# The differential stage as one stream over four heads, with a later tile's projection in pieces between the parts of each attention unit

## What is computed

```python
h = rms_norm(x, norm_g)
z = h @ w_in                        # 1024 -> 4096: ret_q,k,v,gate, diff_q,k,v,gate
# retention group: 4 heads of 128, in chunks of 128 rows with a recurrent state
# differential group: 4 heads; q and k are normed and rotated, in two maps of 64
s = einsum('bqhcd,bkhcd->bhcqk', q, k) * 64 ** -0.5      # c: the two maps, causal
p = softmax(s)
a = p[:, :, 0] - lam * p[:, :, 1]
o_diff = einsum('bhqk,bkhe->bqhe', a, v)
u = concat([rms_norm(o_ret) * silu(rg), rms_norm(o_diff) * (1 - lam_init) * silu(dg)])
y = x + u @ w_out
# sample rows: the same with 4096 cached keys and values each, in pages of 128 found by a table
```

## Time and profile before

| what | us |
| --- | --- |
| median of 3 runs | 2093.59 (2093.02 to 2105.36) |
| the profiled run, device time | 2095.8 |
| its span | 2094.1 |
| TensorE busy | 1702.9 (81%) |
| VectorE busy | 1124.7 (54%) |
| GpSimd busy | 702.4 (34%) |
| ScalarE busy | 675.1 (32%) |

### The profile page before, as it was taken

One profiled execution on the slowest core, in us unless ns is written; L12 is line 12 of the kernel. 1 busy time (PEld: TensorE's weight loads), 2 busy tenths in 40 slices (PEclk: granted clock), 3 DMA queues, 4 the chain that ended last, 5 costly groups with the idle time before them and its releaser, 6 DMA issues. The chain is left out here.

```text
span 2094.1 us, 31531 instructions
## 1 busy us (share of the span) xinstructions
PE 1702.9 (81%) x8316; PEld 1252.9 (60%) x8316; DVE 1124.7 (54%) x2194; ACT 675.1 (32%) x1964; POOL 702.4 (34%) x666
## 2 busy tenths in 40 slices
PE   5859779789799669578895888967889679549998
PEld 1238558568568458356683566845668456418887
DVE  2444533534524528678386783866838768472211
ACT  2321311311311312367233562235632357311100
POOL 1326436446356237211372113730127301140000
PEclk9879999999899889699996999968999789859999
DMA  8866575566566546330464313643136431343432
GB/s 304 302 218 188 165 224 182 178 208 194 168 215 196 181 143 201 120 109 29 133 202 121 106 31 119 201 126 106 42 104 196 131 111 51 84 147 130 136 134 72
DMA packets 185467, 314.54 MB, mean 150 GB/s; under 512 B 17331, under 2 KB 79548, under 8 KB 185156
## 3 DMA queue, kind: packets, MB, share of 16 engines
q1 hardware_dynamic: 176948, 287.22, 44.4%
q0 software_dynamic: 8352, 25.50, 3.2%
HBM read 275.99 MB, written 36.67 MB: 149 GB/s over the span
## 5 line engine op out<-in xcount | busy, mean ns | idle before, releaser
L540 PE MATMUL s_z<-g_w_hi,g_hT 128*128 128x512 f32 x1024 | 406.7, 397 | 43.6 <-DMA s_h_lo<-h_low_scratch 32.3
L542 PE MATMUL s_z<-g_w_hi,s_h_lo 128*128 128x512 f32 x1024 | 410.3, 401 | 0.0
L597 POOL TENSOR_TENSOR s_ring<-s_ring,s_q_row 128x1024 f32<-128x1024 f32 x128 | 321.1, 2510 | 257.3 <-DMA s_ring<-in_cache_k 245.0
L541 PE MATMUL s_z<-g_w_lo,g_hT 128*128 128x512 f32 x1024 | 406.1, 397 | 0.0
L603 DVE TENSOR_REDUCE s_scores<-s_ring 128x16 f32<-128x1024 f32 x128 | 156.2, 1220 | 332.1 <-POOL s_ring L597 320.1
L558 ACT COPY s_zqk<-s_z 128x256 f32<-128x256 f32 x128 | 47.7, 373 | 633.4 <-PE s_z L542 633.4
L540 PEld LDWEIGHTS s_z<-g_w_hi,g_hT 128*128 128x128 f32 x1024 | 195.4, 191 | 91.7 <-DMA s_h_lo<-h_low_scratch 35.5
L1262 ACT ACTIVATE s_weights<-s_sc,s_neg_max 128x512 f32<-128x512 f32 (+3 forms) x320 | 196.5, 624 | 91.4 <-DVE s_neg_max L1401 68.0
L541 PEld LDWEIGHTS s_z<-g_w_lo,g_hT 128*128 128x128 f32 x1024 | 195.4, 191 | 47.9
L542 PEld LDWEIGHTS s_z<-g_w_hi,s_h_lo 128*128 128x128 f32 x1024 | 195.1, 191 | 43.0
L1518 PE MATMUL s_o<-s_vg,s_aT 128*128 128x128 f32 x1088 | 159.8, 296 | 52.7 <-ACT s_aT L1244 48.3
(11 more groups left out here) (205 smaller groups left out, 2744.7 us busy)
## 6 DMA issues: line engine op xcount, KB each, us to landing
s_h_lo<-h_low_scratch SPq DMA_DIRECT2D x131, 512.0 KB, 3.5
s_ring<-in_cache_k SPq DMA_DIRECT2D x256, 256.0 KB, 3.3
s_ring<-in_cache_v SPq DMA_DIRECT2D x256, 256.0 KB, 2.9
w_raw<-in_w_in SPq DMA_DIRECT2D x8, 2048.0 KB, 11.4
s_w_raw<-in_w_in SPq DMA_DIRECT2D x64, 256.0 KB, 3.5
s_u_in<-u_scratch SPq DMA_DIRECT2D x17, 512.0 KB, 3.9
x_in<-in_x_prompt SPq DMA_DIRECT2D x16, 512.0 KB, 6.1
h_low_scratch<-lo_out POOLq DMA_DIRECT2D x16, 512.0 KB, 5.6
```

Of the source, the lines that this page charges most:

```text
L540: pe.matmul(s.z_bank[t % 2][:], hi, g.w_hi[:, c, :], start=(c == 0), stop=False)
L541: pe.matmul(s.z_bank[t % 2][:], hi, g.w_lo[:, c, :], start=False, stop=False)
L542: last = pe.matmul(s.z_bank[t % 2][:], lo, g.w_hi[:, c, :], start=False, stop=(c == DC - 1))
L597: pool.tensor_tensor(slot[:], slot[:], bc(s.q_row[:].unsqueeze(1), [P, 2, 512]), ALU.mult).then_inc(s.keys_times_q, 1)
```

## The change

The loop over heads in the differential stage becomes straight code: 64 tiles (`NTILE`) pass as one stream of steps from -5 to 65. In step n the engines work on the unit T = n and on the projection of tile X = n + 5 (`LEAD`), which may belong to the next head. TensorE does the projection in three pieces, of 3, 3 and 2 chunks, between the parts of the unit.

- One z bank and one turn bank take the place of two that served both.
- Keys' and values' slots become rings of 24 tiles (`VSLOTS`), as two heads overlap.
- Upper h no longer stays in SBUF after retention. Retention writes it to HBM (`h_high`) before its loop, and the differential stage loads both halves, 1 MB a tile, into three slots each. `g.hT` is laid out by tiles.
- The product of cached keys with q moves from GpSimd to VectorE (`use_keys`). Keys stand in steps 0 to 9 of each head (two pairs in the first six, then one), the row's softmax in 9 to 12, the values' eight quads in 12 to 15.
- The next head's weights are loaded whole in advance (`w_raw` holds 8 chunks) and split in steps 10 and 11, as each chunk of the old ones is used for the last time.
- In retention the loads of the next head's first three h tiles move from the loop's start to its end.

The diff, cut: declarations, the unchanged bodies that only lose their loop offset, and the removed code are left out.

```diff
-    rows = slice(t * P, (t + 1) * P)
     for c in range(DC):
-        hi, lo = g.hT[:, c, rows], s.h_lo[t % LSLOTS][:, c, :]
+        hi, lo = g.hT[:, t, c, :], s.h_lo[t % LSLOTS][:, c, :]
...
+            for t in range(LSLOTS):
+                load_low(sp, io, s, g, 0, t)
+            for t in range(NT):
+                sp.dma_start(io["h_high"][t], g.hT[:, t].rearrange("p c x -> p (c x)").bitcast(F32)).then_inc(high_stored, 16)
...
-                for t in range(LSLOTS):
-                    load_low(sp, io, s, g, it, t)
...
+                for t in range(LSLOTS):
+                    load_low(sp, io, s, g, it + 1, t)
+            sp.wait_ge(high_stored, 16 * NT)
+            for t in range(LSLOTS):
+                sp.wait_ge(g.low_loaded[t], low_at(s, NH, t))
...
+LEAD = 5
+NTILE = NH * NT
+UNIT_STEPS = range(-LEAD, NTILE + 2)
+VSLOTS = 24
+KEYS_AT = [2, 2, 2, 2, 2, 2, 1, 1, 1, 1] + [0] * 6
+QUADS_AT = [0] * 12 + [2, 2, 2, 2]
+FIRST_KEY = [sum(KEYS_AT[:i]) for i in range(NT)]
+FIRST_QUAD = [sum(QUADS_AT[:i]) for i in range(NT)]
...
+            def load_h(X):
+                if X >= NTILE:
+                    return
+                if X >= LSLOTS:
+                    sp.wait_ge(tile_used, X - LSLOTS + 1)
+                for dst, src in ((h_hi, "h_high"), (h_lo, "h_low")):
+                    sp.dma_start(dst[X % LSLOTS][:].rearrange("p c x -> p (c x)").bitcast(F32), io[src][X % NT]
+                                 ).then_inc(h_loaded[X % LSLOTS], 16)
+
...
+            for X in range(2):
+                load_h(X)
+            load_q(0)
+            for n in UNIT_STEPS:
+                load_h(n + LEAD + 2)
+                if n % 2 == 0 and 0 <= (n + 2) // 2 < NPAIRS:
+                    store_kv((n + 2) // 2)
+                h, i = row_step(n + 1)
+                if 0 <= h < NH:
+                    for j in range(FIRST_KEY[i], FIRST_KEY[i] + KEYS_AT[i]):
+                        load_pages(h, j)
+                    for j in range(2 * FIRST_QUAD[i], 2 * (FIRST_QUAD[i] + QUADS_AT[i])):
+                        load_pages(h, NPAIR + j)
+                    if h + 1 < NH and 1 <= i < 1 + DC:
+                        load_weights(h + 1, i - 1)
+                    if h + 1 < NH and i == 14:
+                        load_q(h + 1)
...
+            def keep_z(X):
...
+                act.wait_ge(tile_used, X + 1)
+                act.copy(zqk[b % 3][:, X % 2, :], z_bank[:, 0:2 * P])
+                act.copy(vg[:, X % VSLOTS, :], z_bank[:, 2 * P:4 * P])
+                act.activation(th[b % 2][:, X % 2, :], z_bank[:, 3 * P:4 * P], ACT.Tanh, scale=0.5).then_inc(z_kept, 1)
...
+            for n in UNIT_STEPS:
+                X, T, b = n + LEAD, n, (n + 2) // 2
+                new_head = (X + 1) // NT if (X + 1) % NT == 0 and X + 1 < NTILE else 0
+                for k in unit_groups(T - 2)[1]:
+                    keep_turned(("a", k))
+                if n % 2 == 0 and 0 <= b < NPAIRS:
+                    key_high(b)
+                h, i = row_step(n)
+                if i == 12 and 0 <= h < NH:
+                    act.wait_ge(row_dve, h * ROW_DVE + 4)
+                    act.activation(scores, scores, ACT.Exp, scale=QSCALE).then_inc(row_exp, 1)
+                if 0 <= T < NTILE:
+                    exps(T, 0)
+                if new_head:
+                    for c in range(0, 3):
+                        weights_high(new_head, c)
+                if 0 <= T - 2:
+                    square_output(T - 2)
+                if n % 2 == 1 and 0 <= n + 1 < NTILE:
+                    keep_turned(("k", (n + 1) // 2))
+                if 0 <= T + 1 < NTILE:
+                    keep_turned(("q", T + 1))
+                if new_head:
+                    for c in range(3, 6):
+                        weights_high(new_head, c)
+                if X < NTILE:
+                    keep_z(X)
+                    if X % 2 == 1:
+                        square(X // 2)
+                if new_head:
+                    for c in range(6, DC):
+                        weights_high(new_head, c)
+                for k in unit_groups(T - 1)[0]:
+                    keep_turned(("a", k))
+                if 0 <= T < NTILE:
+                    exps(T, 1)
...
+            def use_keys(h, j):
+                dve.wait_ge(q_loaded, 16 * (h + 1))
+                dve.wait_ge(ring_loaded[j % RING], ring_at(h, j))
+                slot = ring[j % RING]
+                chain.link(dve.tensor_tensor(slot[:], slot[:], bc(q_row[:].unsqueeze(1), [P, 2, 512]), ALU.mult))
+                dve.tensor_reduce(scores[:, 2 * j:2 * j + 2, :], slot[:].rearrange("p i (s f) -> p i s f", f=DH),
+                                  AX, ALU.add).then_inc(keys_used, 1)
...
+            for n in UNIT_STEPS:
+                X, T = n + LEAD, n
+                h, i = row_step(n)
+                new_head = (X + 1) // NT if (X + 1) % NT == 0 and X + 1 < NTILE else 0
+                now_head = X // NT if X % NT == 0 and 0 < X < NTILE else 0
+                keys = list(range(FIRST_KEY[i], FIRST_KEY[i] + KEYS_AT[i])) if 0 <= h < NH else []
+                if n % 2 == 1 and 0 <= (n + 3) // 2 < NPAIRS:
+                    square_sums((n + 3) // 2)
+                if 0 <= T < NTILE:
+                    find_bias(T, 0)
+                if 0 <= T + 1 < NTILE:
+                    split_q(T + 1)
+                if 0 <= T - 1 < NTILE:
+                    find_coef(T - 1)
+                    combine(T - 1)
+                if 0 <= T - 2:
+                    gate_output(T - 2)
+                if new_head:
+                    for c in range(0, 3):
+                        weights_low(new_head, c)
+                if now_head:
+                    for c in range(6, DC):
+                        weights_low(now_head, c)
+                if n % 2 == 0 and 0 <= (n + 2) // 2 < NPAIRS:
+                    key_low((n + 2) // 2)
+                if i == 0 and h >= 1:
+                    row_heads(h - 1)
+                if i == 12 and 0 <= h < NH:
+                    row_sums(h)
+                for j in keys[:1]:
+                    use_keys(h, j)
+                if 0 <= T < NTILE:
+                    find_bias(T, 1)
+                if n % 2 == 1 and 0 <= (n + 3) // 2 < NPAIRS:
+                    norm_and_rope((n + 3) // 2)
+                    halve_gate((n + 3) // 2)
+                if new_head:
+                    for c in range(3, 6):
+                        weights_low(new_head, c)
+                for j in keys[1:]:
+                    use_keys(h, j)
+                if 0 <= h < NH:
+                    if i == 9:
+                        row_largest(h)
+                    if i == 10:
+                        row_bias(h)
+                    if i == 11:
+                        row_shift(h)
+                if h >= 1:
+                    if i == 0:
+                        row_total(h - 1)
                     if i == 1:
+                        row_result(h - 1)
...
+            def project(X, chunks):
+                if X >= NTILE:
+                    return
+                h = X // NT
+                if chunks[0] == 0:
+                    if X >= 1:
+                        pe.wait_ge(z_kept, X)
+                    pe.wait_ge(h_loaded[X % LSLOTS], 32 * (X // LSLOTS + 1))
+                hi, lo = h_hi[X % LSLOTS], h_lo[X % LSLOTS]
+                for c in chunks:
+                    if X % NT == 0 and h >= 1:
+                        pe.wait_ge(w_low, (h - 1) * DC + c + 1)
+                    pe.matmul(z_bank[:], hi[:, c, :], g.w_hi[:, c, :], start=(c == 0), stop=False)
+                    pe.matmul(z_bank[:], hi[:, c, :], g.w_lo[:, c, :], start=False, stop=False)
+                    last = pe.matmul(z_bank[:], lo[:, c, :], g.w_hi[:, c, :], start=False, stop=(c == DC - 1))
+                    if c == DC - 1:
+                        last.then_inc(tile_used, 1)
+                    elif X % NT == NT - 1:
+                        last.then_inc(w_free, 1)
+
...
+            def turn(job):
+                kind, k = job
+                n = JOB[job]
+                if n >= 1:
+                    pe.wait_ge(turn_kept, n)
...
+            for n in UNIT_STEPS:
+                X, T = n + LEAD, n
+                h, i = row_step(n)
+                if 0 <= T < NTILE:
+                    score(T, 0)
+                project(X, range(0, 3))
+                turn_and_weigh(T - 2, unit_groups(T - 2)[1])
+                if 0 <= T < NTILE:
+                    score(T, 1)
+                if n % 2 == 1 and 0 <= n + 1 < NTILE:
+                    turn(("k", (n + 1) // 2))
+                project(X, range(3, 6))
+                if 0 <= h < NH:
+                    if i == 10:
+                        pe.wait_ge(row_dve, h * ROW_DVE + 1)
+                        pe.transpose(row_bank[0:HC, 0:P], row_max[:], g.ident[:]).then_inc(row_pe, 1)
+                    if i == 11:
+                        pe.wait_ge(row_dve, h * ROW_DVE + 3)
```

(13 more changed lines are left out.)

819 lines of the change are left out of this document (422 added, 397 removed).

## The result

The changed kernel takes 2024 us (median) against 2098 us for the kernel before on the same chip. The ratio is 0.9637, with a 95% interval of 0.9589 to 0.9686: faster by 3.6%. One of the changed kernel's four runs took 2116 us at a granted clock of 0.806, where the other three have 0.931 to 0.936, and the ratio leaves it out. The prediction was 2046 us, range 1992 to 2112, faster with a chance of 0.62.

The account below looks back on a forecast made before the run. TensorE's projection, waits in the attention units' ring over three engines, and 32 us of fill and drain per head were taken to bound the differential stage. Span 2094.1 - 62 (stage) + 15 (retention) = 2047, median 2046 us, range 1992 to 2112.

Parts of the forecast that it names:

- the prologue: Start of the differential stage: five steps with projection alone, 33 us, plus 2 for the first tile's two halves of h.
- the last head with the closing steps: End of the differential stage: 210 us for a head partly without projection, plus 13 for two closing steps.
- Steps 0 to 7: Narrow steps of each head: VectorE taken as the bound, 101 us together against 106 before.
- Sum 11.0, with waits 11.6 to 12: VectorE's time in us per narrow step: key pairs 5.1, unit work 3.8, norm, rope and the rest 2.1.
- the bound of 2.51 us: Narrow steps: upper price of one key product on VectorE, its time on GpSimd; 1.22 us was taken.
- Steps 8 to 15: Wider steps of each head: 63 us for 8 to 11 and 80 for 12 to 15, against 61 and 64.
- the walk: Differential stage: a step's time added up link by link through TensorE's in-order queue and ScalarE's copies, 20.9 us for unit 14.
- The rival that it would fall: Narrow steps: clock drops to 0.75, adding 67 us over 24 steps, 2113 us in all; chance 0.13.
- Longer hops: Differential stage: three more hand-overs, 0.75 us in each of 64 steps, add 48 us, giving 2094; chance 0.20.
- The product at GpSimd's price: Narrow steps: VectorE's key product costs 1.3 us more, 62 us in all, giving 2108; chance 0.05.
- the stream overlaps better than walked: Retention loads pass the stores, saving 15 us, and each stage step sheds 0.65, saving 42, giving 1990; chance 0.20.
- The stall: Retention's first head: 16 stores of h's upper half delay the fourth tile's load; 15 us, between bounds 0 and 27.

Follow-up runs that it names:

- e10: Changed kernel with VectorE's product of cached keys with q left out and put nowhere else; one run, differential stage 944 us against 952.
- e4: Changed kernel with a tile's eight chunks projected as one block instead of three pieces; ratio 1.0013 to the kernel before, stage 1038 us.
- e1: Changed kernel with the 16 stores of h's upper half issued on ScalarE's DMA queue instead of SP's; ratio 0.9568 to the kernel before.
- e6: e1 with the next head's first three loads moved back to the start of the retention loop; ratio 0.9566 to the kernel before.
- e5: Changed kernel loading only an eighth of h's lower half per tile after the first three in the differential stage; ratio 0.9615 to before.

## Why the prediction was right, and where its steps failed

**The direction and the bound.** That the change takes the gaps of the units and the 32 us of fill and drain, and that its pieces stand in TensorE's queue, was right; so were the prologue (35.6 us against 35) and the last head with the closing steps (221 against 223). Of the 38 us by which the stage came out shorter, all lie in the first three heads: 223.6 + 236.1 + 235.5 = 695 against 732.

**The first head.** Its steps 0 and 1 took 7.4 and 9.4 us, against 14.6 and 13.2 in the second, as no wide units lie before them: 11 us that the sum charged by taking three equal heads. Both facts stood in the prediction; the sum forgot one.

**Steps 0 to 7: right in size, wrong in cause.** 101 forecast, 96 measured. The term "Sum 11.0, with waits 11.6 to 12" for VectorE failed in steps 2 and 3: VectorE has 18.4 us of work in the two, 9.2 a step, and they took 9.5 and 9.8. The term took the mean of units 2 to 5 for every step, but the work is uneven, 9.0 to 12.7 us a step in steps 2 to 6. And VectorE did not set them alone (e10), though it was 95% busy, the very figure that the prediction had named as the proof. In steps 4 to 6 it did set part, 3 us of 36.5. The key product itself was priced well:

```profile
L1561 DVE TENSOR_REDUCE s_scores<-s_ring 128x16 f32<-128x1024 f32 x64 | 78.1, 1220 | 2.2
L1560 DVE TENSOR_TENSOR s_ring<-s_ring,s_q_row 128x1024 f32<-128x1024 f32 x64 | 78.0, 1219 | 0.4
```

1219 ns against the 1.22 taken, and the bound of 2.51 us was far off.

**Steps 8 to 15.** 63 and 80 forecast, 62 and 78 measured, by the mechanism named: the second map's exponentials wait for the turned weights' copy. A tile in the wide steps is not hidden: in the last head, whose steps 11 to 14 have no projection, they take 12.4, 14.6, 13.4 and 13.9 us against 15.1, 19.1, 18.4 and 20.4 in the second head, 2.7 to 6.5 for a tile that costs 5.75 alone.

**What the walk missed.** It got the sum of a step right with the pieces where they were, and e4 shows that it would have given the block the same time, 86 us too little. It did not see that idle hand-overs, many of them 0.68 us, are what the pieces remove, nor that without the pieces the clock falls.

**The clock.** Taken at full speed, measured 1.00 in steps 0 to 7 and 12 to 15. The rival that it would fall was wrong for this kernel, and e4 shows how near it was: with the same work in one block it was 0.92 in steps 0 to 7. The Trainium skill (TensorE: Matmul & The Clock Gate, Part 1), which the prediction cited, makes throttled the default and activity what releases it, so that a TensorE that idles falls back; e4's trace agrees. In steps 0 to 7 e4's longest wait, 1.6 us, is no longer than the changed kernel's 1.8; it has 25 waits against 15.

**The rivals.** Longer hops would have made a head 256 us, against 236. The product at GpSimd's price is out. That the stream overlaps better than walked came half true: each of the narrow steps was 0.6 us shorter on the mean, but the fourth tile's load still waited behind the stores.

**Retention.** The stall was 13.5 us against 15, for the reason given: queue order for 10 of it (e1). Two sizes in it were off: the DMA engines at full moved 418 GB/s and not 313, and the clock's fall after the wait, some 3 us, was not in the sum. Another 9 us of retention lie outside the sum: 2 were expected and put into the prologue (from the end of TensorE's last product with value pages to the stage's first projection, 17.8 before and 19.5 after), and most of the rest is late value pages (TensorE waits 10.5, 11.7 and 11.1 us for them in the first three heads, 9.9, 8.6 and 8.2 before), unexplained. That the moved loads change nothing held (e6), as did the stream at no cost (e5).
